# A hybrid attention and expert-lookup step on one core: cache pages by gathers of four pages, and the prompt attention of the last two tiles moved behind the first 112 expert gathers

## The reference

```python
u, cq, ckv, kr, qx, gates = split(rmsnorm(x) @ w_in)
pool_y = pool_mix(u, hist)                               # branch 1
q = rmsnorm(cq) @ w_q_up ; c_kv = rmsnorm(ckv)           # branch 2
prompt: for each 128-token tile i of 4, each of 8 heads:
    s = q . k[:L], L = 128 * (i + 1), causal mask; softmax; @ v[:L]
sample: lat_past = cache_kv_latent[page_table]           # 8 samples x 16 pages x 128 rows x 256
        kr_past  = cache_k_rope[page_table]              # x 32
        scores over 2048 + 4 rows, softmax, @ latents, @ w_uv
mem_o = memory_attention(qx, mem_k, mem_v)               # branch 3
h = x + (sum of sigmoid(gate) * (branch @ w_out)) @ w_o
q = rmsnorm(h) @ w_peer_q ; top 16 + 16 keys -> top 16 pairs per head -> idx[token, 128], gate
a = gelu(h . peer_u[idx]) ; y = h + sum_k gate_k * a_k * peer_v[idx_k]
```

## Time and profile before

| | |
|---|---|
| median of 3 runs | 2369.8 us (2367.28 to 2374.38) |
| the profiled execution | 2363.25 us, span 2361.5 us |
| PE busy | 1403.1 us (59%) |
| DVE busy | 1196.7 us (51%) |
| POOL busy | 1110.4 us (47%) |
| ACT busy | 403.7 us (17%) |
| DMA | 687.35 MB, mean 291 GB/s |
| mean granted TensorE clock | 0.765 |

### The profile page before, as it was taken

One profiled execution on the slowest core, in us unless ns is written; L12 is line 12 of the kernel. 1 busy time (PEld: TensorE's weight loads), 2 busy tenths in 40 slices (PEclk: granted clock), 3 DMA queues, 4 the chain that ended last, 5 costly groups with the idle time before them and its releaser, 6 DMA issues.

```text
span 2361.5 us, 22207 instructions
## 1 busy us (share of the span) xinstructions
PE 1403.1 (59%) x6922; PEld 806.3 (34%) x6922; DVE 1196.7 (51%) x2862; ACT 403.7 (17%) x1227; POOL 1110.4 (47%) x1225
## 2 busy tenths in 40 slices
PE   7997787999887578765766333333333333322348
PEld 5875545788775445442433000000000000000012
DVE  2104324511147976468567566576575575674400
ACT  2213223510112121102212101101101101011000
POOL 0004510000024456556666666666666666666662
PEclk9998897999998789886887655555655565565679
DMA  6214633045359899999999999999999999999995
GB/s 200 72 64 130 166 105 125 1 139 158 125 200 329 316 393 377 390 341 380 399 397 371 366 375 363 366 373 375 365 371 369 367 361 375 379 364 369 369 369 189
DMA packets 269164, 687.35 MB, mean 291 GB/s; under 512 B 36039, under 2 KB 119912, under 8 KB 269039
## 3 DMA queue, kind: packets, MB, share of 16 engines
q0 software_dynamic: 161792, 579.94, 65.3%
q1 hardware_dynamic: 107255, 106.00, 14.1%
HBM read 681.84 MB, written 4.18 MB: 290 GB/s over the span
## 4 chain that ended last, share of the span: by engine, by line
PE 28%; POOL 23%; issue 13%; DMA 13%; DVE 9%; another core or an unknown queue 8%; SPq 4%; ACT 1%; DVEq 1%; ACTq 0%; POOLq 0%
POOL arena L638 23%; PE bank L669 20%; DMA arena<-in_peer_u_dram,arena 7%; DVE arena L1867 5%; PE bank L1147 5%; DMA arena<-in_peer_v_dram,arena 3%; PE bank L665 2%; DVEq L1803 1%; SPq L513 1%; SPq L509 1%; SPq L510 1%; DMA arena<-in_x_sample_dram 1%; DMA arena<-in_w_pool_out_dram 1%; DMA arena<-in_w_mla_out_dram 1%
## 5 line engine op out<-in xcount | busy, mean ns | idle before, releaser
L1147 PE MATMUL bank<-arena 128*32 128x512 f32 x2176 | 480.7, 949 | 788.7 <-DMA arena<-in_peer_v_dram,arena 730.8
L1867 DVE CUSTOM_DVE_ANT_0 arena<-arena,bank 128x1024 f32<-128x1024 f32 x544 | 655.2, 1220 | 413.4 <-DMA arena<-in_peer_u_dram,arena 378.5
L638 POOL DMA_INDIRECT arena<-in_peer_u_dram,arena x544 | 518.2, 952 | 617.6 <-DVE arena L1852 391.1
L669 PE MATMUL bank<-arena 128*128 128x256 f32 (+7 forms) x2940 | 712.9, 400 | 94.4 <-DVE arena L1769 26.8
L638 POOL DMA_INDIRECT arena<-in_peer_v_dram,arena x544 | 521.8, 959 | 372.9 <-remote 156.3
L669 PEld LDWEIGHTS bank<-arena 128*128 128x128 f32 (+2 forms) x2940 | 547.2, 195 | 268.4 <-issue 108.3
L1147 PEld LDWEIGHTS bank<-arena 128*32 128x32 f32 x2176 | 98.0, 147 | 1139.3 <-issue 1138.3
L1178 ACT ACTIVATE arena<-bank 128x256 f32<-128x256 f32 (+12 forms) x321 | 124.6, 418 | 435.7 <-PE bank L669 167.0
L665 PE MATMUL bank<-arena 128*128 128x128 f32 (+4 forms) x766 | 121.7, 307 | 58.1 <-DMA arena<-in_cache_k_rope_dram 16.9
L630 POOL DMA_DIRECT2D arena<-in_cache_kv_latent_dram x64 | 34.6, 541 | 229.4 <-issue 229.4
L1178 ACT ACTIVATE arena<-arena 32x8 f32<-32x8 f32 x544 | 115.8, 213 | 128.6 <-issue 57.2
(11 more groups left out here) (142 smaller groups left out, 853.5 us busy)
## 6 DMA issues: line engine op xcount, KB each, us to landing
arena<-in_w_in_dram SPq DMA_DIRECT2D x30, 1024.0 KB, 5.8
arena<-in_w_peer_q_dram SPq DMA_DIRECT2D x16, 1024.0 KB
arena<-in_peer_u_dram,arena POOLq DMA_INDIRECT x544
arena<-in_peer_v_dram,arena POOLq DMA_INDIRECT x544
arena<-in_cache_kv_latent_dram POOLq DMA_DIRECT2D x64, 128.0 KB
arena<-in_cache_kv_latent_dram SPq DMA_DIRECT2D x64, 128.0 KB, 2.1
arena<-in_w_o_dram SPq DMA_DIRECT2D x8, 1024.0 KB
arena<-in_cache_mem_k_dram SPq DMA_DIRECT2D x8, 512.0 KB, 5.1
```

The source lines that it names most:

```text
L638: pool.indirect_dma_start(out=ring[s % RING], out_offset=None, in_=table[0], in_offset=IndirectOffsetOnAxis(ap=ix, axis=0)).then_inc(land[ ...
L669: last = pe.matmul(dst, lhs(k), rhs(k), start=(k == 0), stop=(k == n - 1))
L1147: last = pe.matmul(bank[rows_out, c], zw[:, n % 2, QW // 4 * j + m], ring[at_slot[j] % RING][:, c * 512:(c + 1) * 512], start=(first and m ...
L1867: dve.tensor_tensor_reduce(ring[s % RING], ring[s % RING], h_dot, 1.0, 0.0, ALU.mult, ALU.add, act_a[:, n % 2, k:k + 1]).then_inc(u_free, 1)
```

## The change

- **Pages**: SP no longer loads pages. POOL issues, for each step, four indirect gathers of 128 rows of 4 KB (each 128 rows are 4 pages, cut into 32 chunks of 4 tokens) and four of 128 rows of 512 bytes (rope keys). The row numbers `pidx` are computed by 7 small DVE instructions at the start, from a page table now loaded to all 128 partitions. The rope keys land in `rop` (2 buffers) and ACT reorders them into `rop_j`, one copy a step. The second sample's memory rows now load after step 7's scores instead of after `pv_mm` 6.
- **Attention**: `ATT` runs 16 `"mla"` units of tiles 0 and 1 and the 16 `"mem"` units ahead; the 16 units with L = 384 and 512 become `late()`, a background in front of `part(1)`, due at ticks 30, 33, ... 87. They use a copy of the queries that POOL makes and keep `kT`, `vtm` in place.
- **Ring**: because those tiles lie where buffers 0 to 10 of the ring were, the first `FRONT` = 112 gathers run in 11 other buffers: gather s waits for gather s - 11. From gather 112 the ring is the 14 buffers, moved by 10.75 KB.
- **part(1)**: all its ticks are 108 later (112 + 3h instead of 4 + 3h), and SP starts to load its weights only when the first 112 gathers are used up.

```diff
-ATT = [("mla", q, h, P * (q + 1)) for q in range(4) for h in range(H)]
+ATT = [("mla", q, h, P * (q + 1)) for q in range(2) for h in range(H)]
 ATT += [("mem", q, h, MEM) for q in range(4) for h in range(XH)]
+AHEAD = len(ATT)
+ATT += [("mla", q, h, P * (q + 1)) for q in range(2, 4) for h in range(H)]
+FRONT = 112
+EARLY_SLOTS = (11, 12, 13) + tuple(range(RING, RING + 8))
+SLOT = [EARLY_SLOTS[s % len(EARLY_SLOTS)] if s < FRONT else (s - FRONT + 13) % RING for s in range(len(ORDER))]
-    ticks = [4 + 3 * h for h in range(2 * MERGE)]
-    ticks += [152 + 4 * r for r in range(12)]
+    ticks = [30 + 3 * k for k in range(LATE + 4)]
+    ticks += [FRONT + 3 * h for h in range(2 * MERGE)]
+    ticks += [FRONT + 148 + 4 * r for r in range(12)]
...
# SP
-            for s in range(STEPS):
-                load_pages(s)
...
+            sp.wait_ge(u_free, EARLY_U)
+            sp.wait_ge(v_free, EARLY_V)
             for m in range(MPAIRS):
                 load_merge(1, m)
# POOL
+            def pages(s):
+                for j in range(4):
+                    pool.indirect_dma_start(out=lat[s % 3][:, j].rearrange("p r d -> p (r d)"), out_offset=None, in_=lat_rows,
+                                            in_offset=IndirectOffsetOnAxis(ap=pidx[:, 4 * (s // 4) + j, s % 4:s % 4 + 1],
+                                                                           axis=0)).then_inc(land[s % 3], 16)
...
+            pages(0)
+            pages(1)
+            pool.wait_ge(pool_mm, 2 * PG)
+            pool.wait_ge(pool_d, PG)
+            ropes(0)
+            ropes(1)
+            pages(2)
+            for s in range(2, STEPS):
                 if s >= 3:
                     pool.wait_ge(pv_mm, s - 2)
+                    pages(s)
+                pool.wait_ge(rp_ev, s - 1)
+                ropes(s)
...
+                if s == FRONT:
+                    pool.wait_ge(at_xm, len(GROUPS))
# ACT, in the page steps
+                act.wait_ge(ld_rope[s % 2], 64 * (s // 2 + 1))
+                copy(rop_j.rearrange("p r (j d) -> p j r d", j=4),
+                     rop[:, s % 2].rearrange("p j (r d) -> p j r d", r=ROWS)).then_inc(rp_ev, 1)
# TensorE; DVE and ACT have a late() of the same shape
+                for k in range(LATE + 4):
+                    if k < LATE:
...
+                        pe.matmul(bank[:, 4 + k % 2, 0:L], late_q[0:QD, h, (q - 2) * P:(q - 1) * P], kT[0:QD, h, 0:L],
+                                  start=True, stop=True).then_inc(at_mm, 1)
...
+                    yield
-            bg = Background(part(1))
+            bg = Background(one_by_one(late(), part(1)))
```

More of the change, by code:

```diff
@@ L1 @@
 from contextlib import ExitStack
+from itertools import chain as one_by_one
 import concourse.bass as bass
 from concourse import mybir
-from concourse.bass import DynSlice, IndirectOffsetOnAxis
+from concourse.bass import IndirectOffsetOnAxis
 ALU = mybir.AluOpType
@@ L34 @@
 PGRP = 4
+CHUNK = 32
+ROWS = PAGE // CHUNK
 LATW = KL + ROPE
@@ L397, in hybrid_step @@
         land = [sem(f"land{i}") for i in range(RING)]
-        land0 = [16 * 16 * len(range(i, STEPS, 3)) if i < 3 else 0 for i in range(RING)]
+        land0 = [64 * len(range(i, STEPS, 3)) if i < 3 else 0 for i in range(RING)]
+        late_in = sem("late_in")
         (tk_gap, tk_exp, id_next, idvf, idv_done, gelu_done, w_done, wv_done, z_done, u_free, v_free, acc_free) = map(
@@ new lines, in ropes @@
+            def ropes(s):
+                for j in range(4):
+                    pool.indirect_dma_start(out=rop[:, s % 2, j], out_offset=None, in_=rope_rows,
+                                            in_offset=IndirectOffsetOnAxis(ap=pidx[:, 4 * (s // 4) + j, s % 4:s % 4 + 1],
+                                                                           axis=0)).then_inc(ld_rope[s % 2], 16)
+            pages(0)
+            pages(1)
+            pool.wait_ge(pool_mm, 2 * PG)
+            pool.wait_ge(pool_d, PG)
@@ L637, in gather @@
+            pool.wait_ge(qt_ev, 2 * TILES)
+            pool.wait_ge(ms_mm, NB)
+            pool.wait_ge(st_pool, 16 * (NB + 1))
+            pool.tensor_copy(late_q[0:QD], qT[0:QD, :, 2 * P:4 * P]).then_inc(late_in, 1)
             def gather(s, table, ix):
-                pool.indirect_dma_start(out=ring[s % RING], out_offset=None, in_=table[0],
-                                        in_offset=IndirectOffsetOnAxis(ap=ix, axis=0)).then_inc(land[s % RING], 16)
+                pool.indirect_dma_start(out=ring[SLOT[s]], out_offset=None, in_=table[0],
+                                        in_offset=IndirectOffsetOnAxis(ap=ix, axis=0)).then_inc(land[LAND[s]], 16)
```

231 lines of the change are left out of this document (154 added, 77 removed).

## The result

The changed kernel takes 2384.5 us (median of 5 runs, 2382.96 to 2396.97) against 2369.2 us of the kernel before in the same comparison: ratio 1.0069, 95% interval 1.0046 to 1.0091. The forecast was 2334 us, range 2314 to 2357. Its profiled execution took 2382.96 us, span 2381.1; the kernel before's span was 2361.5, so the two traces have 19.6 us between them to explain.

The account below looks back on a forecast made before the run. Transfers bind the steady gathers, DVE's list gathers 0 to 64, POOL's loads the page steps, TensorE the attention ahead. Terms -25 - 33 - 12 + 34 = -36 us gave a median of 2334 us, range 2314 to 2357.

Parts of the forecast that it names:

- Page steps: Page stage before the attention: eight steps take 87 us instead of 111.5, 25 us gained, bounds 28 and 14.
- Rival 5: Page steps: POOL's gathers each wait for a DVE copy or reduction, 12 us more than before, 2371 us; chance 0.03.
- Attention: Ahead of the first expert gather: attention of the L = 384 and 512 units leaves the chain, 33 us gained (31 to 34).
- Front: Gathers 0 to 112: gather 112 comes at 197 us instead of 209.1, 12 us gained; bounds 15 gained, 11 lost.
- The late units: Gathers 0 to 112, DVE's list: 7 units cost 7.5 us up to gather 64, 6 with two rescalings 9 us later.
- The ring: Gathers 64 to 112: 11 buffers lose about 1 us in each of 6 groups, so 200 instead of 194.5 us.
- rival 2: Gathers 0 to 112: ring of 11 paces the front, 3 us a group, 18 us of gain lost, 2352 us; chance 0.16.
- part(1) behind: After gather 112: 15.7 MB of merge weights moved to where transfers bind, at 2.2 us a MB, 34 us lost (28 to 40).
- Slower: Whole kernel slower than before, 2382 us, through late units holding up weighings in the front; chance 0.05.
- rival 3: Front: late units stand before each weighing in TensorE's list; at 8 us a group 48 us lost, 2382 us; chance 0.05.

Follow-up runs that it names:

- the kernel with direct pages: Changed kernel with only the pages undone: SP and POOL load whole pages as before, no rope copy; 2366.1 us, ratio 0.9974 to the kernel before.
- the wait ahead of gather 5: Kernel before with one wait added on POOL's queue: gather 5 waits for part(0)'s last query product; 2365.8 us against 2371.5, ratio 0.9967.

## Why the prediction was wrong

- **Page steps, -25 forecast, +18: the step that failed.** "So 13 + 7 x 10.6 = 87 us": POOL's 9.9 us a step and TensorE's 10.6 were both right, and with four gathers a step TensorE did run at 10. The sum took for granted that two engines below their limits don't touch each other. Eight gathers in a row delay the signals on which TensorE, ACT and DVE take turns in four PSUM buffers, and a step becomes 16 to 20 us. The bounds (28 and 14) had no term for it. Some 6 us of the 18 are slower TensorE work: it was busy 85.4 us in 208 to 323 us before and 91.8 us in 208 to 341 us now, the granted clock 0.86 and 0.82 there.
- **Rival 5 named the right culprit by the wrong mechanism.** It priced a page stage 12 us longer, 2371 us. POOL's gathers kept their 0.94 to 0.95 us beside these steps, so the rule of the Trainium skill ("SBUF — State Buffer", A bandwidth-pool intuition that's wrong) on descriptors locked out by DVE does not show here. The row that would have told was in the trace of before and was not read: ACT waiting 14.2 us for a late signal beside the first 14 gathers.
- **Attention, -33: right ahead of the first gather**, -36.6 from the last page scores to gather 0, a little more than its bound of 34. The time it frees is paid again behind.
- **Front, -12 forecast, +3.** The late units were priced about rightly (16 of 1.05 us and two rescalings on DVE, some 18 us; 13.5 measured). The ring was mis-sized: "about 1 us lost in each of 6 groups"; 28.2 us of waits in 5 groups, and +11.5 us net by difference. That is the mechanism of rival 2, which put it at 18 us. Gather 64 came out close by luck (126 forecast, 123.4): before's 34.6 us up to the first product were taken over as fixed and held 8.7 us of late signal, and from the first product on it took 97.5 us instead of the 91.4 of the sum. Gathers 64 to 112 then took 89.1 us instead of 71.
- **part(1) behind, +34: right where it was done alone**, 112 to 464 33.9 us longer (573.9 us, forecast 574); in the changed kernel 25.5, under the lowest bound of 28. The same stretch took 561 to 571 us in ten traces with the same work there, so single traces don't tell the two apart for certain. By the 358 GB/s of the Trainium skill ("SBUF — State Buffer", Summary: rules for kernel authors) it would have been an estimated 44; this trace moved 386 GB/s in that stretch.
- **Slower** had 0.05, for rival 3, whose late units do stand in front of the first weighing, but cost 13.5 us and not 48.

Without the page term the forecast would have been -11 and the kernel with direct pages measured -6 (ratio 0.9974), no more than what the wait ahead of gather 5 gives alone (0.9967).

Not settled: whether TensorE's instructions really end late or only their signals do. The ends in the trace are modelled. The Trainium skill ("Perfetto Trace Analysis", Tensor Engine Instruction) says the same of the profiler's end, and that the semaphore update is pushed when PSUM has acknowledged all bytes; a hold-up of either kind would look like these rows.

Nor is it TensorE alone. DVE's signals are on time in the page steps, but beside the expert gathers of the changed kernel one comes 4.9 us after its instruction's end (741.64, signal 746.52). DVE goes on with its next products meanwhile, and POOL waits:

```profile
741.55 0.08 DVE L1995 DVE_READ_ACCUMULATOR2_ANT arena<- 128x1 f32 x1
742.69 0.08 DVE L1995 DVE_READ_ACCUMULATOR2_ANT arena<- 128x1 f32 x1
746.78 0.93 POOL L658 DMA_INDIRECT arena<-in_peer_u_dram,arena  x1 [5.86 <-remote]
```

DVE's ends are not modelled ones, which speaks for the signals being late and not the work. Which engine is hit when, and by what, is open.

## What to carry to other kernels

Keep POOL's indirect gathers in short rows beside work that hands over between engines often: up to four in a row cost little here (10 us a step, signals up to 3.1 us late), eight made a 10 us step 16 us long. Before adding gathers to a stage, read the waits on "remote" in the trace of before, wherever gathers already run; one such wait is a price. And work that leaves the critical path into a stage that is itself bound (DVE's list, the ring, transfers) has to be priced there in full: 40 us gained ahead came back as 34 behind.

## What the runs showed of the hardware

- Beside back-to-back indirect gathers from POOL, signals of TensorE arrive up to 8.8 us after the modelled end in step 1 (221.64, signal 230.43), one in 1.4 to 2.9 us, and those piled up follow at 0.06 us intervals 1.8 to 3 us after the last gather's issue ends. Gathers of 64 KB do it too (118.1 us of stage, against 131.6 where four of the eight are of 512 KB); 104 plain loads from POOL did not. In gathers 0 to 64 of the changed kernel it was up to 4.9 us for DVE's signals.
- It runs through the whole lookup: from 1448 to 2256 us 53 of 66 weighings signal over 0.5 us late, up to 4.0 us, and POOL waits 114.2 us in all on "remote". With the DMA engines at 0.97 there, what that costs is not shown.
- Idle time put into the gather queue can make a start faster in which other engines hand over to each other: 10.5 us of waiting, first product 8.7 us sooner.
- A load with a register load from SP's queue costs 1.12 us with one DMA and 1.62 us with two, so 16 separate small loads a step (17.9 us) were worse here than eight gathers (stage 155.7 and 131.6 us).
